# Value slabs computed with stationary weights and transposed afterwards, and both heads' probability copies on ScalarE, in a two-block fp32 transformer kernel

## The reference

```python
# block 1, layer 0: 12 query heads on 4 key/value heads of 64, window of 128, a sink logit,
# and 4 more heads on 256 memory tokens
h = rmsnorm(x, norm_mix[i]);  proj = h @ w_in_a[li]
q, k, v, qm = jnp.split(proj, [qw, qw + kvw, qw + 2 * kvw], axis=-1)
y_tok = windowed_gqa(q, k, v, sink_a[li])
# block 1, layer 1: the same with 12 key/value heads and a learnt bias on a grid (neighbourhood_attn)
y_mem = memory_attn(qm, mk, mv)
x = x + jnp.concatenate([y_tok, y_mem], axis=-1) @ w_out[i]
...
# block 2 (16 meta tokens ahead: 528 tokens), layer 1: 16 query heads on 4 key/value heads
q = rms_norm((h @ wq), q_norm_w) * (d ** -0.5);  k = rms_norm((h @ wk), k_norm_w);  v = h @ wv
p = sink_softmax(logits, sink);  o = p @ v
```

## Time and profile before

| | |
|---|---|
| median of 3 runs | 2857.73 us (2857.48 to 2858.75) |
| the profiled execution | 2859.37 us |
| its span in the trace | 2857.6 us |
| mean granted PE clock | 0.947 of full speed |
| PE busy | 2714.1 us, 95% |
| ACT, DVE, POOL busy | 935.8, 1041.6 and 1198.0 us |
| HBM read | 209.57 MB, 74 GB/s over the span |

### The profile page before, as it was taken

How to read it: one execution, slowest core, us unless ns; L and a number is a source line. 1 busy time by engine, 2 the same in 40 slices (tenths; PEclk the granted TensorE clock), 3 DMA queues, 4 the chain that set the end, 5 groups by cost and what they waited for, 6 DMA issues and landing times.

```text
span 2857.6 us, 50530 instructions
## 1 busy us (share of the span) xinstructions
PE 2714.1 (95%) x18058; PEld 2404.4 (84%) x18058; DVE 1041.6 (36%) x1918; ACT 935.8 (33%) x2090; POOL 1198.0 (42%) x1007
## 2 busy tenths in 40 slices
PE   7989999999988999999997778999999899999998
PEld 7857888888966888888996668999999767999998
DVE  3273221221055321236635653432432354442340
ACT  4274322232166322234331113322233354322231
POOL 4444444444363444444423214444444332444343
PEclk9999999999999999999987888999999855999999
DMA  4121232232131222232211001222222100222222
GB/s 164 65 51 52 96 105 85 91 102 88 60 56 39 92 95 92 95 105 89 88 53 37 1 1 59 89 95 82 90 102 74 45 1 9 88 88 96 88 95 82
DMA packets 80384, 213.16 MB, mean 75 GB/s; under 512 B 30224, under 2 KB 32912, under 8 KB 80272
## 3 DMA queue, kind: packets, MB, share of 16 engines
q1 hardware_dynamic: 80272, 211.69, 22.2%
HBM read 209.57 MB, written 2.10 MB: 74 GB/s over the span
## 4 chain that ended last, share of the span: by engine, by line
PE 89%; DVE 5%; issue 2%; POOL 2%; ACT 1%; DVEq 0%; DMA 0%; POOLq 0%; SPq 0%; ACTq 0%
PE ps L1084 72%; PE ps L1099 4%; PE ps L1309 3%; PE ps L1227 2%; PE ps L1210 2%; PE ps L1197 2%; DVE s_sb L1471 1%; PE ps L1231 1%; POOL bias_sb L616 1%; PE ps L1279 1%; ACT s_sb L829 1%; DVE p_t L1456 0%; DVE x_t L1446 0%; DVE x_m L1446 0%; DVEq L1424 0%
## 5 line engine op out<-in xcount | busy, mean ns | idle before, releaser
L538 POOL TENSOR_TENSOR w_lo<-raw,w_hi 128x512 fp32r<-128x512 f32 (+1 forms) x704 | 977.1, 1410 | 1232.0 <-ACT w_hi L730 1232.0
L730 ACT ACTIVATE w_hi<-raw 128x512 fp32r<-128x512 f32 (+1 forms) x704 | 426.5, 653 | 1430.9 <-PE ps L1084 1315.6
L1084 PE MATMUL ps<-h_hi,w_hi 128*128 128x264 f32 (+1 forms) x3296 | 872.4, 321 | 15.2 <-POOL h_lo L684 8.4
L1084 PE MATMUL ps<-h_lo,w_hi 128*128 128x264 f32 (+1 forms) x3296 | 870.3, 320 | 0.0
L1084 PE MATMUL ps<-h_hi,w_lo 128*128 128x264 f32 (+1 forms) x3296 | 868.2, 320 | 0.0
L1084 PEld LDWEIGHTS ps<-h_hi,w_hi 128*128 128x128 f32 x3296 | 550.2, 189 | 65.0 <-issue 16.9
L1084 PEld LDWEIGHTS ps<-h_lo,w_hi 128*128 128x128 f32 x3296 | 546.8, 189 | 45.4 <-issue 1.0
L1084 PEld LDWEIGHTS ps<-h_hi,w_lo 128*128 128x128 f32 x3296 | 547.4, 189 | 43.6
L1084 PE MATMUL ps<-act_lo,w_hi 128*128 128x264 f32 (+1 forms) x1056 | 282.3, 322 | 0.0
L1084 PE MATMUL ps<-act_hi,w_lo 128*128 128x264 f32 (+1 forms) x1056 | 282.0, 321 | 0.0
L1084 PE MATMUL ps<-act_hi,w_hi 128*128 128x264 f32 (+1 forms) x1056 | 280.9, 320 | 0.0
(11 more groups left out here) (228 smaller groups left out, 2851.7 us busy)
## 6 DMA issues: line engine op xcount, KB each, us to landing
raw<-slabs_d SPq DMA_DIRECT2D x288, 512.0 KB, 3.2
raw<-slabs_d SPq DMA_DIRECT2D x64, 704.0 KB, 4.0
rpb_raw<-rpb_d SPq DMA_DIRECT2D x24, 224.0 KB, 5.0
bias_sb<-alibi_d SPq DMA_DIRECT2D x6, 384.0 KB, 3.3
x<-x_d SPq DMA_DIRECT2D x1, 2048.0 KB, 13.2
out_d<-x SPq DMA_DIRECT2D x1, 2048.0 KB, 7.4
mem_in<-mem_d SPq DMA_DIRECT2D x1, 1024.0 KB, 7.3
dn_cst<-dn_consts_d SPq DMA_DIRECT2D x1, 640.0 KB, 5.1
```

The costliest lines, as they stand in the source:

```text
L538: nc.gpsimd.tensor_tensor(w_lo[:, s, a * P:b * P], raw[:, s, a * P:b * P], w_hi[:, s, a * P:b * P].bitcast(f32), ALU.subtract).then_inc(lo ...
L730: nc.scalar.activation(w_hi[:, s, a * P:b * P], raw[:, s, a * P:b * P], ACT.Copy)\
L1084: last = nc.tensor.matmul(ps[:, s * 2 * BANK + po:s * 2 * BANK + po + n], w[:, s, wk], a[:, k, to:to + n], start=(k == 0 and w is w_hi and ...
```

## The change

Four things are altered.

1. **Value slabs** use `slab`, as queries and keys do. DVE scales the result with `rstd` along the free axis into a new buffer `v_f` (two tiles, features on partitions). PE then transposes it in blocks of 128 tokens (`turn_values`: four transposes a slab, five in the fourth layer) into PSUM banks 4 to 7, and DVE copies it to `val` (`keep`: one copy, in the fourth layer a second one of 16 rows).
2. **The order of slabs.** In layers 0 and 1 the value slabs now come first; each is transposed behind the next slab. In the fourth layer they stay last, and both are transposed after the last slab. POOL waits for `val_kept` before it stages values, and prepares queries and keys of the first tile when all but the last two slabs are done.
3. **`turn_root`** and the copy to `rstd_col` go from the three projection stages that have values. The memory projection and the third layer keep them.
4. **ScalarE copies both heads'** transposed probabilities. DVE's `turned` is gone. In ACT's step the copy of head 0 stands ahead of head 0's exponential, the copy of head 1 between the two exponentials.

```diff
@@ gpsimd, attend @@
                     else:
                         for s in range(RING):
-                            pool.wait_ge(acc_free[s], (st.slab0 - nv) // 2)
+                            pool.wait_ge(acc_free[s], (st.slab0 - 2) // 2)
                     chores[0](0)
                     chores[1](0)
                     chores[3](0)
-                    for s in range(RING):
-                        pool.wait_ge(acc_free[s], st.slab0 // 2)
+                    pool.wait_ge(val_kept, st.val0)
                     chores[2](0)
@@ scalar, attend @@
-                def turned(p):
+                def turned(p, h):
...
-                    act.wait_ge(pt_done, 2 * p.count + 1)
+                    act.wait_ge(pt_done, 2 * p.count + h + 1)
...
                 def step(p):
-                    if p.back(1).exists:
-                        turned(p.back(1))
                     for h in range(2):
+                        if p.back(1).exists:
+                            turned(p.back(1), h)
                         probs(p, h)
@@ tensor @@
+            def turn_values(st, q, i, s):
+
+                pe.wait_ge(acc_free[s], q + 1)
+                for j, (t0, n) in enumerate(COLS[st.blk]):
+                    last = nc.tensor.transpose(ps[0:n, (4 + 2 * s) * BANK + j * P:(4 + 2 * s) * BANK + (j + 1) * P],
+                                               v_f[:, s, t0:t0 + n], ident)
+                last.then_inc(val_turned, 1)
@@ tensor, proj_heads @@
-                slab_tokens(q0 + n, 0, toks, hi, lo)
+                slab(q0 + n, 0, st.blk, hi, lo)
                 mean_squares(st, n - 1)
-                slab_tokens(q0 + n, 1, toks, hi, lo)
+                slab(q0 + n, 1, st.blk, hi, lo)
+                for s in range(RING):
+                    pe.wait_ge(tn_rt, st.tn0 + st.nf - 1 + s)
+                    turn_values(st, q0 + n, 0, s)
@@ tensor, proj @@
+                first_pair(st, st.blk, hi, lo, cols=False)
+                for i in range(1, nv + 1):
+                    for s in range(RING):
+                        slab(q0 + i, s, st.blk, hi, lo)
+                        turn_values(st, q0 + i - 1, i - 1, s)
+                many(q0 + nv + 1, st.nf // 2 - 1, st.blk, hi, lo)
@@ vector, proj @@
+                def v_tile(i, s):
+                    ended(i + q1, s)
+                    scaled(halves_of(v_f[:, s, span(st.blk)], st.blk), acc(s, st.blk), st.pre).then_inc(acc_free[s], 1)
+
+                def keep(i, s):
+                    wait(val_turned, st.val0 + 2 * i + s + 1)
+                    f = slice((2 * i + s) * P, (2 * i + s + 1) * P)
+                    last = copy(val[st.h][:, 0:4, f], bank(4 + 2 * s).rearrange("p (b n) -> p b n", b=4))
+                    if st.blk == 2:
+                        last = copy(val[st.h][0:META, 4, f], bank(5 + 2 * s)[0:META, 0:P])
+                    last.then_inc(val_kept, 1)
...
                     v_tile(0, 0)
+                    norm_pair(st.nf // 2 - 1)
                     v_tile(0, 1)
+                    for s in range(RING):
+                        keep(0, s)
+                    return
```

More of the change, by code:

```diff
@@ L73, in plan @@
     out = []
-    c = dict(slab=0, pair=0, tile=0, tn=0, ffn=0, col=0)
+    c = dict(slab=0, pair=0, tile=0, tn=0, ffn=0, col=0, val=0)
     kinds, norms = [], []
@@ L94, in proj @@
         slabs(nf + nv, UP)
-        c["col"] += 1
+        c["val"] += nv
     def att(**kw):
@@ L286, in build @@
         v_st = small("v_st", [P, 2, 5, P])
+        v_f = small("v_f", [P, 2, TOK], f32, 6304)
         sq = small("sq", [P, 2, TOK], f32, 7400)
@@ L880, in attend @@
                 last = last_pair(st)
-                turned(last)
+                for h in range(2):
+                    turned(last, h)
                 spread(last)
@@ L1571, in proj @@
                             norm_pair(i - 1)
[L1572 to L1573 removed]
                         f_tile(i, 1)
[L1575 to L1592 removed]
                     v_tile(0, 0)
[L1594 to L1595 removed]
+                    norm_pair(st.nf // 2 - 1)
                     v_tile(0, 1)
[L1597 to L1600 removed]
+                    for s in range(RING):
+                        keep(0, s)
+                    return
+                for s in range(RING):
+                    v_tile(0, s)
+                for i in range(1, st.nv // 2):
+                    for s in range(RING):
+                        keep(i - 1, s)
+                        v_tile(i, s)
+                for i in range(st.nf // 2):
+                    for s in range(RING):
+                        f_tile(i, s)
+                        if i == 0:
+                            keep(st.nv // 2 - 1, s)
             def attend(st):
@@ L1639, in invert @@
                     recip(p_inv[0:p.nq, p.slot, :], p_sum[0:p.nq, p.slot, :]).then_inc(inv_ready, 1)
-                def turned(p):
-                    cs = p.c["chunks"]
-                    full = sum(1 for ch in cs if ch[1] == P)
-                    wait(pt_done, 2 * p.count + 2)
-                    if counted(p.count - 1):
-                        wait(pv_done, p.count - 1)
-                    src = bank(5).rearrange("p (c n) -> p c n", n=P)
-                    last = None
-                    if full:
-                        last = copy(p_t[:, p.slot, 1, 0:full, 0:p.nq], src[:, 0:full, 0:p.nq])
-                    if full < len(cs):
-                        last = copy(p_t[0:META, p.slot, 1, full, 0:p.nq], src[0:META, full, 0:p.nq])
-                    last.then_inc(pt_ready[1], 1)
                 def normalise(p):
```

61 lines of the change are left out of this document (14 added, 47 removed).

## The result

| | before | changed |
|---|---|---|
| median, first comparison | 2857.6 us (2854.6 to 2858.8) | **2792.3 us** (2789.9 to 2792.8) |
| ratio, 95% interval | | 0.977 (0.975 to 0.978) |
| medians, a later comparison | 2857.4 us | 2789.8 us, ratio 0.976 (0.975 to 0.978) |
| profiled execution, span | 2857.6 us | 2788.1 us |
| mean granted PE clock | 0.947 | 0.948 |

The kernel became faster by 65 us where 48 were forecast.

What follows compares the result with a forecast made beforehand. It took PE to bound the projections and the fourth layer's attention (at 1.2 GHz), and a loop through all engines the first two attentions. Terms summed to -48.9 us from 2859.4, giving 2810 us, range 2800 to 2826.

Steps and rivals of the forecast that it cites:

- Value slabs: First two layers' projections: eight value slabs fall from 10.70 to 5.57 us plus 0.6 for transposes, gaining 36.2 us.
- turn_root and the fourth layer's projection: Three projections lose tiny matmuls, 2.1 us gained; fourth layer's two value slabs shorten, net 10.6 us after an open tail.
- The alibi pairs: First layer's attention, 24 pairs: VectorE's relief shortens each by 0.2 us, -5 us; ends -8 and +10.
- ScalarE's floor of 2.75 us: Alibi pairs: 3.1 less 0.78 of gaps plus 0.43 for the second copy, leaving up to 0.35 a pair to win.
- The grid bias: 24 attention pairs: ScalarE's work rises from 2.82 to 3.40 us, 0.1 a pair lost, +2 us; ends 0 and +14.
- Memory pairs: 16 attention pairs: the second copy stands on the loop, +0.3 us for 13 of them, +4 us; ends 0 and +6.
- Starts: First layer's attention: second tile prepared about 3 us earlier, -1 us, between -3 and +2; second layer 0.
- The fourth layer's attention: 40 pairs: PE stays the bound at 1.2 GHz after the same sink-logit block, so the extra copies cost 0.
- the rival of 2772: Fourth layer's attention stays at full clock because the sink logit slips between POOL's splits, 38 us less; chance 0.07.
- The second layer at 1.2 GHz: Rival: second layer's attention falls to 1.2 GHz for its whole length, 66 us more, 2876; chance 0.04.
- The prediction's last sentence: If the clock is as before and time is off by over 10 us, the second copy's place on ACT was mis-sized.

Runs made afterwards that it cites:

- the copies alone: Kernel before with only this change: ScalarE copies both heads' transposed probabilities, VectorE's copy gone; five executions about 2845 us, five about 2818, ratio 0.990.
- a *third* copy: Changed kernel with ScalarE copying head 1's transposed probabilities a second time into a buffer that nothing reads; 2807.7 us.
- the slabs alone: Changed kernel with VectorE copying head 1's transposed probabilities again and ScalarE head 0's alone; 2804.2 us.
- the reduce: Changed kernel with the sink logit written by a one-input VectorE tensor_reduce instead of a two-input tensor_tensor, first and fourth layer; median 2783.2 us.

## Why the prediction was wrong, point by point

**Value slabs: right.** The chain in the second layer's projection, where two value slabs are turned:

```profile
644.40 0.44 PE ps L1162 x4
644.84 5.57 PE ps L1086 x24
650.41 0.44 PE ps L1162 x4
```

Four transposes are 0.44 us, forecast 0.6; the trace's 0.52 for four was the nearer figure. A value slab is 6.01 us in place of 10.70. Eight of them save 37.5 (36.2 forecast). In these two layers the chain shows no wait of the transposes for VectorE. The estimate of 1.1 us from the Trainium skill, "TensorE: Matmul & The Clock Gate", section "Part 4: PE-mode transpose", is not borne out: the 0.44 measured here is 0.11 a transpose.

**turn_root and the fourth layer's projection: right.** 0.7 a projection fits both tables. There the last slab is followed by the open tail that was worked out: transposes at 2188.65 and 2189.71, copies from 2189.65 to 2191.83, which is 3.0 us behind the slab's end, and the stage after it is 1.9 us longer. (Here the second slab's transposes do wait 0.35 us for VectorE's scaling.)

**The alibi pairs: the term that failed.** 0.2 us a pair was forecast, 0.7 came (3.10 to 2.38), and the stage is 13.6 us shorter with the copies alone, where -5 stood. The mechanism was named rightly (waits for VectorE, which loses its copy), the bound was not. Two steps were wrong. The first was ScalarE's floor of 2.75 us, too high by three things. It took the length of ScalarE's row, 0.43, for what a copy costs; from start to start it is 0.26 to 0.37. And it took 3.1 less the listed gaps for ScalarE's work, but waits of 0.16 for VectorE's second minimum are listed as no gap: an exponential of 385 columns starts 0.76 before the next in the kernel with VectorE's copy (165.31 to 166.07), and 0.60 before its successor in the changed one (159.49 to 160.09). And a listed gap begins only at the end of the row before it: in the kernel before, the high part starts 0.57 after the start of the copy of the result (165.13 to 165.70), which takes 0.16 where nothing waits (161.25 to 161.41), so that wait is 0.41 and 0.32 is listed. An estimate with the three put right is 2.75 - 0.11 - 0.16 - 0.09 = 2.39; the real floor is 2.38.

The second error then was to take 0.2 of the 0.35 that was left, without a reading of VectorE's own timeline. From the reciprocal to the instruction behind the copy it has 0.84 and 0.97 us (166.20 to 167.04, and 169.24 to 170.21 with three chunks), without a copy 0.26 (159.62 to 159.88 in the changed kernel). So a pair with little slack loses 0.58 or 0.71, on average 0.65 of the 0.72 that came.

In the changed kernel the stage is 15.5 us shorter: 16.3 between the first and the last alibi pair's transpose, 0.1 ahead of them, and 0.9 longer in the memory part. Some of the 16.3 is the clock, which at the stage's start was at 1.2 GHz for 3.4 us in place of 10.2.

**The grid bias: sign wrong, +2 where -5.8 came** (82.5 to 76.8 us from the first pair to the last). The same two errors: ScalarE's floor with the second copy was put at 3.40, and with a *third* copy it measures 3.42, so it is about 2.94. And PE without gaps was read as PE being the bound at 3.29, where VectorE paced it at 3.28; PE alone needs 3.20, which is 24 x 0.08 = 2 us (an estimate). That the tile goes at the pace of the mask's loop was right. That one copy more would lengthen this loop was wrong: VectorE's copy lay on it, and ScalarE's doesn't. Masks now start every 14.2 us in place of the 15.1 of the earlier trace rows, as the chain shows, and six tiles at 0.9 are 5.3 of the 5.8 us, the 2 us included.

```profile
780.31 4.14 POOL bias_sb L618 x2
...
794.54 4.14 POOL bias_sb L618 x2
```

**Memory pairs: right**, 0.27 against 0.3, undone and measured.

**Starts: -1 forecast, about -1.2 found** in the kernel with the slabs alone; the other 1.6 us by which its first attention is shorter go with the clock in the memory part.

**The fourth layer's attention: right in its outcome, its cause not.** It stayed at 1.2 GHz, with 4.89 us of block. But the forecast and the rival of 2772 both had the block decide, and without it the clock falls too; in the changed kernel it falls 0.2 us before the block begins. What does decide stays open: the copies alone run at two levels 27 us apart, and the reduce had a full clock for the last fifth of the stage in its profiled execution. That the lower level comes from this stage was not shown.

**The second layer at 1.2 GHz: did not come.** PE's gaps there grew no larger: it is busy for 97.8 of 113.4 us, before for 99.0 of 114.3, at a clock of 0.95 and 0.96. (The 6.2 us that the prediction had for such a pair is an estimate that no row shows.)

The prediction's last sentence named the second copy's place on ScalarE as what to suspect if the clock was as before. The place is worth nothing (2790.2 against 2789.8). What failed is what the copy was said to cost ScalarE and to free on VectorE.

## What to carry to other kernels

Before work is moved from one engine to another, read the timeline of the engine that is relieved over one period of the loop: if it has no gap above some 0.16 us, as VectorE here, it may be the pace-setter, whatever its busy share says and however full the engine looks that you had in mind. A timeline without gaps is no proof, for PE's had none in the grid-bias pairs and VectorE paced them. Price an added instruction by the distance to the next start in a full stretch, not by its row's length. And check the guess of who sets the pace by one idle copy more on each engine, and by the distance between the starts of whatever a tile waits for.

## What the runs showed of the hardware

- A ScalarE row is longer than the time it takes the engine, by different amounts at the same starts: a copy of 128x256 has a row of 0.37 us in the kernel with the copies alone and of 0.49 in the one with one copy more, each 0.26 to the next start.
- Four fp32 transposes of 128x128 between slabs take 0.44 us at full clock, from 644.40 to 644.84.
- A two-input tensor_tensor of two elements beside four GpSimd splits stood for 4.89 us, a reduce in its place for 0.16.
- The granted clock can take different courses in executions of one kernel (0.948 and 0.961 on average, 27 us apart).
- At the start of the fourth layer's attention the clock fell at 2193.1 in the changed kernel, with PE's pause of 4.79 us still to come, and at 2190.0 in the kernel with the reduce, which has no such pause.
